# A hybrid decoder step on one core: RWKV's chunk matrices as 64-row blocks, and cache page numbers read sixteen at a time

## The reference, cut to what matters

```python
def step(S, inp):
    r_t, w_t, k_t, v_t, kk_t, a_t = inp
    sa = jnp.einsum('bhij,bhj->bhi', S, -kk_t)
    S = (S * w_t[:, :, None, :] + sa[..., None] * (kk_t * a_t)[:, :, None, :]
         + v_t[..., None] * k_t[:, :, None, :])
    return S, jnp.einsum('bhij,bhj->bhi', S, r_t)
```

```python
k_past = cache_k[l][page_table].reshape(bs, past_len, N_HEADS, HEAD_DIM)
z = jnp.einsum('bqhd,bkhd->bhqk', q, k) * (HEAD_DIM ** -0.5) + sb_bias
log_keep = jnp.where(causal, jax.nn.log_sigmoid(-z), 0.0)
after = lax.cumsum(log_keep, axis=3, reverse=True) - log_keep
A = jnp.where(causal, jnp.exp(jax.nn.log_sigmoid(z) + after), 0.0)
```

## Time and profile before

| | |
|---|---|
| median of 3 runs | 3560.51 us (3560.0 to 3560.63) |
| profiled execution, its own time | 3560.32 us |
| its span in the trace | 3558.6 us |
| TensorE busy | 3362.0 us, 94% of the span |
| VectorE, ScalarE, GpSimd busy | 27%, 13%, 17% |
| granted TensorE clock, mean | 0.97 |

### The profile page before, as it was taken

One profiled execution on the slowest core, in us unless ns is written; L12 is line 12 of the kernel. 1 busy time (PEld: TensorE's weight loads), 2 busy tenths in 40 slices (PEclk: granted clock), 3 DMA queues, 4 the chain that ended last, 5 costly groups with the idle time before them and its releaser, 6 DMA issues.

```text
span 3558.6 us, 39904 instructions
## 1 busy us (share of the span) xinstructions
PE 3362.0 (94%) x16700; PEld 2682.7 (75%) x16700; DVE 955.1 (27%) x1950; ACT 463.6 (13%) x778; POOL 600.5 (17%) x613
## 2 busy tenths in 40 slices
PE   6999998979999989999989999898799999899999
PEld 4777776657888778888857777775588877688887
DVE  3222002344333223331032220123343432333300
ACT  2001003302111111000010000123031101100000
POOL 3333000320000013440023320002200000144300
PEclk8999999989999999999989999999899999999999
DMA  6343332331110222213153433323311112122121
GB/s 265 142 153 115 121 120 75 125 98 50 45 45 30 78 83 71 83 60 105 62 213 142 155 118 113 124 82 97 98 47 45 45 45 75 71 83 83 56 82 66
DMA packets 61711, 335.27 MB, mean 94 GB/s; under 512 B 10592, under 2 KB 10976, under 8 KB 32480
## 3 DMA queue, kind: packets, MB, share of 16 engines
q1 hardware_dynamic: 46656, 295.40, 22.5%
q0 software_dynamic: 12320, 33.57, 3.1%
q10 hardware_dynamic: 2560, 3.80, 0.3%
HBM read 326.71 MB, written 6.02 MB: 94 GB/s over the span
## 4 chain that ended last, share of the span: by engine, by line
PE 86%; issue 3%; ACT 3%; DVE 3%; DMA 2%; POOLq 2%; POOL 1%; SPq 0%; DVEq 0%; ACTq 0%
PE ps L544 85%; DMA ring<-w_ada 2%; POOLq L514 1%; ACT ws L1125 1%; ACT u L1125 1%; DMA ws<-cache 1%; POOL ws L516 1%; DVE ws L1360 1%; ACT L1125 1%; DVE y L1360 0%; POOLq L516 0%; PE ps L954 0%; DVE proj L1360 0%; DVE ws L1764 0%; DVE x L1363 0%
## 5 line engine op out<-in xcount | busy, mean ns | idle before, releaser
L544 PE MATMUL ps<-u,ring 128*128 128x272 f32 x4864 | 1210.4, 400 | 57.4 <-ACT u L1125 51.1
L544 PEld LDWEIGHTS ps<-u,ring 128*128 128x128 f32 x4864 | 918.7, 193 | 283.1 <-ACT u L1125 53.8
L544 PE MATMUL ps<-proj,ring 128*128 128x272 f32 x3328 | 771.2, 394 | 9.4 <-DVE proj L1360 9.4
L544 PEld LDWEIGHTS ps<-proj,ring 128*128 128x128 f32 x3328 | 632.9, 191 | 146.9 <-DVE proj L1360 12.0
L1360 DVE TENSOR_TENSOR ws<-ws,ps 128x272 f32<-128x272 f32 (+3 forms) x570 | 269.3, 476 | 1167.1 <-PE ps L544 1158.3
L528 POOL TENSOR_TENSOR masked_room<-ring 128x512 f32<-128x512 f32 x44 | 55.8, 1267 | 1590.4 <-DMA ring<-w_up 1361.1
L544 PE MATMUL ps<-y,ring 128*128 128x272 f32 x1216 | 312.4, 393 | 0.5 <-DVE proj L1360 0.5
L1125 ACT ACTIVATE ws<-ps 128x272 f32<-128x272 f32 (+5 forms) x374 | 163.1, 443 | 1056.2 <-PE ps L544 974.3
L516 POOL DMA_DIRECT2D ws<-cache x256 | 137.5, 537 | 828.6 <-issue 828.6
L544 PEld LDWEIGHTS ps<-y,ring 128*128 128x128 f32 x1216 | 231.4, 191 | 49.8 <-DVE proj L1360 2.0
L544 PE MATMUL ps<-y,masked_room 128*128 128x272 f32 x1056 | 258.4, 395 | 0.3 <-DVE y L1360 0.2
(11 more groups left out here) (191 smaller groups left out, 1910.2 us busy)
## 6 DMA issues: line engine op xcount, KB each, us to landing
ring<-w_up SPq DMA_DIRECT2D x88, 1024.0 KB, 4.8
ring<-w_ada SPq DMA_DIRECT2D x72, 1024.0 KB, 5.3
ring<-w_down SPq DMA_DIRECT2D x64, 704.0 KB, 4.1
ws<-cache POOLq DMA_DIRECT2D x256, 128.0 KB, 2.3
ring<-w_gate SPq DMA_DIRECT2D x32, 1024.0 KB, 4.8
ring<-w_in SPq DMA_DIRECT2D x22, 1024.0 KB, 4.9
ring<-w_branch SPq DMA_DIRECT2D x32, 256.0 KB, 4.6
ring<-w_out SPq DMA_DIRECT2D x8, 1024.0 KB, 5.0
```

The lines of the kernel that those rows point to most:

```text
L544: return nc.tensor.matmul(out, lhsT, rhs, start=start, stop=stop, skip_group_check=skip)
```

## The change

There are two parts.

**Blocks of 64 rows.** The RWKV matrices are stored as 4 heads of 64 columns: rows 0 to 63 hold the block of chunk 0, rows 64 to 127 that of chunk 1, and nothing is stored of the masked halves. Each call of `heads` (4 products of 128 rows) becomes `by_chunk` (8 products of 64 rows by 64 columns, on rows 0-63 and rows 64-127 in turn, both into one PSUM bank at their own partitions) or `by_channel` (8 products whose 64 rows are the channels of one head, results of the two row halves in two banks). Because a product now reads only one head's 64 channels, `AtP`, `RtP` and `BtP` with their copies and clears are gone. The results that DVE masks and ACT copies are 256 columns instead of 512. The four transposes in groups 6 and 8 become 8 products with the identity (`turn_chunks`). In the chunk groups the products with `LakT` and `MF` take 64 rows instead of 128. The last group goes from 8 products of 128 columns to 16 of 64. The constants are cut to suit. The sample's products follow the same scheme.

**Page numbers in registers.** `cache_loads` reads the 16 page numbers of a turn before it waits for the first slot, and then for each slot waits and issues four DMAs from the registers.

```diff
                 def cache_loads(first, last):
-                    for n in range(first, last):
-                        kv, odd, hf, s = n // 16, n // 8 % 2, n // 4 % 2, n % 4
-                        pool.wait_ge(cache_used.sem, cache_used.upto(l, n - 3))
-                        for pg in range(4):
-                            at_ = (2 * s + odd) * NPAGE + (NPAGE - 1 - (4 * hf + pg))
-                            page = pool.value_load(pages[0:1, at_:at_ + 1], min_val=0, max_val=NPHYS - 1)
-                            dst = cache[:, s, pg, :]
-                            pool.dma_start(dst, cache_d[kv * (DEPTH * NPHYS) + l * NPHYS + page])\
-                                .then_inc(cache_loaded[s].sem, 16)
+                    for n0 in range(first, last, 4):
+                        numbers = [[page_number(n, pg) for pg in range(4)] for n in range(n0, n0 + 4)]
+                        for n in range(n0, n0 + 4):
+                            kv, s = n // 16, n % 4
+                            pool.wait_ge(cache_used.sem, cache_used.upto(l, n - 3))
+                            for pg in range(4):
+                                pool.dma_start(cache[:, s, pg, :],
+                                               cache_d[kv * (DEPTH * NPHYS) + l * NPHYS + numbers[s][pg]])\
+                                    .then_inc(cache_loaded[s].sem, 16)
...
-                def heads(b, lhsT, rhs, n=P, rows=P):
+                def by_chunk(b, lhsT, rhs):
                     for h in range(NH):
-                        m = mm(ps[0:rows, b, h * n:h * n + n], lhsT(h), rhs(h))
+                        for c in range(2):
+                            rows = slice(CH * c, CH * c + CH)
+                            m = mm(ps[rows, b, h * CH:h * CH + CH], lhsT[rows, h, :], rhs[rows, h, :])
                     return m
+                def by_channel(b, n, lhsT, rhs):
+                    for ft in range(2):
+                        for c in range(2):
+                            for q in range(2):
+                                r, rows, at = slice(HD * q, HD * q + HD), slice(CH * c, CH * c + CH), n * P + ft * CH
+                                m = mm(ps[rows, b + q, at:at + CH], lhsT[r, ft, rows], rhs[r, ft, rows])
+                    return m
...
-                    heads(0, ft_of(Bt), hd_of(AtP))
-                    heads(1, ft_of(At), hd_of(BtP)).then_inc(rw_pe.sem, 1)
-                    heads(2, ft_of(Kt_), hd_of(AtP))
-                    heads(3, ft_of(Bt), hd_of(RtP))
+                    by_channel(0, 0, Bt, At)
+                    by_channel(0, 1, At, Bt).then_inc(rw_pe.sem, 1)
+                    by_channel(2, 0, Kt_, At)
+                    by_channel(2, 1, Bt, Rt)
...
-                    heads(0, hd_of(MD), hd_of(ME))
-                    heads(1, hd_of(MD), hd_of(MC))
-                    heads(7, hd_of(MC), hd_of(MD)).then_inc(rw_pe.sem, 1)
+                    by_chunk(0, MD, ME)
+                    by_chunk(1, MD, MC)
+                    by_chunk(7, MC, MD).then_inc(rw_pe.sem, 1)
...
-                        heads(0, hd_of(ET), hd_of(xa))
-                        for h in range(NH):
-                            m = nc.tensor.transpose(ps[:, 1, h * P:h * P + P], xa[:, h, :], cmat(IDENT))
-                        m.then_inc(rw_pe.sem, 1)
+                        by_chunk(0, ET, xa)
+                        turn_chunks(1, xa).then_inc(rw_pe.sem, 1)
...
                             for h in (2 * ft, 2 * ft + 1):
-                                mm(ps[rows, 0, h * HD:h * HD + HD], LakT[:, h, rows],
-                                   vt[:, h * HD:h * HD + HD], start=h % 2 == 0, stop=False, skip=True)
+                                mm(ps[rows, 0, h * HD:h * HD + HD], LakT[rows, slot(h), :],
+                                   vt[rows, h * HD:h * HD + HD], start=h % 2 == 0, stop=False, skip=True)
                             m = mm(ps[rows, 0, ft * P:ft * P + P], At[:, ft, rows], sbd[:, ft, :],
                                    start=False, skip=True)
...
-                    for h in range(NH):
-                        ft, po = h // 2, HD * (h % 2)
-                        o = ps[po:po + HD, 6, 256 + ft * P:256 + ft * P + P]
-                        c2 = slice(h * HD, h * HD + HD)
-                        mm(o, sat[:, c2], MrbT[:, h, :], start=False, stop=False, skip=True)
-                        m = mm(o, vt[:, c2], MrkT[:, h, :], start=False, skip=True)
+                    for v, w in ((sat, MrbT), (vt, MrkT)):
+                        for h in range(NH):
+                            ft, po = h // 2, HD * (h % 2)
+                            for c in range(2):
+                                rows, at = slice(CH * c, CH * c + CH), 256 + ft * CH
+                                m = mm(ps[po:po + HD, 6 + c, at:at + CH], v[rows, h * HD:h * HD + HD],
+                                       w[rows, slot(h), :], start=False, stop=v is vt, skip=True)
...
-                for o, i in ((AtP, At), (RtP, Rt), (BtP, Bt)):
-                    o = o.rearrange("p (f q) n -> p f q n", f=2)
-                    for q in range(2):
-                        r = slice(64 * q, 64 * q + 64)
-                        m = V.tensor_copy(o[r, :, q, 0:n], i[r, :, 0:n])
```

More of the change, by code:

```diff
@@ L48 @@
 IN_ORDER = (8, 9, 10, 3, 0, 1, 2, 4, 5, 6, 7)
-(IDENT, ONES, BLK, TRI, CAUS, CNEG, M16U, M16L, E32L, E64L, SU64, LE64) = [P * i for i in range(12)]
-S4U = 12 * P
+(IDENT, ONES, BLK, TRI, CAUS, CNEG) = [P * i for i in range(6)]
+(M16U, M16L, E32L, E64L, SU64, LE64, ID64) = [6 * P + CH * i for i in range(7)]
+S4U = 6 * P + 7 * CH
 S4L, LE4 = S4U + TS, S4U + 2 * TS
@@ L302, in build @@
         wb = masked_room[:, :]
[L303 to L306, removed]
+        E64 = wb[:, 0:256].rearrange("p (h n) -> p h n", h=4)
+        LakT = wb[:, 256:512].rearrange("p (h n) -> p h n", h=4)
+        MrbT = wb[:, 512:768].rearrange("p (h n) -> p h n", h=4)
+        MrkT = wb[:, 768:1024].rearrange("p (h n) -> p h n", h=4)
         xtf = xt2.rearrange("p f n -> p (f n)")
@@ L889, in _, with turn_chunks, small, small_heads @@
                 fills(5, 8)
-                def heads(b, lhsT, rhs, n=P, rows=P):
+                def by_chunk(b, lhsT, rhs):
                     for h in range(NH):
-                        m = mm(ps[0:rows, b, h * n:h * n + n], lhsT(h), rhs(h))
-                    return m
[L898 to L902, removed]
+                        for c in range(2):
+                            rows = slice(CH * c, CH * c + CH)
+                            m = mm(ps[rows, b, h * CH:h * CH + CH], lhsT[rows, h, :], rhs[rows, h, :])
+                    return m
+                def by_channel(b, n, lhsT, rhs):
[5 more added lines that the diff above has]
+                    return m
+                def turn_chunks(b, v):
+                    for h in range(NH):
+                        for c in range(2):
+                            rows = slice(CH * c, CH * c + CH)
+                            m = mm(ps[rows, b, h * CH:h * CH + CH], v[rows, h, :],
+                                   cst[rows, IDENT + CH * c:IDENT + CH * c + CH])
+                    return m
+                def small(n, lhsT, rhs):
+                    for ft in range(2):
+                        for q in range(2):
+                            r, at = slice(HD * q, HD * q + HD), n * 2 * TS + ft * TS
+                            m = mm(ps[0:TS, q, at:at + TS], lhsT[r, ft, 0:TS], rhs[r, ft, 0:TS])
+                    return m
+                def small_heads(b, lhsT, rhs):
+                    for h in range(NH):
+                        m = mm(ps[0:TS, b, h * TS:h * TS + TS], lhsT[0:TS, h, 0:TS], rhs[0:TS, h, 0:TS])
+                    return m
                 for tt in range(NTT):
@@ L928, in _ @@
                     pe_.wait_ge(rw_dve.sem, tile_dve(2))
-                    heads(0, hd_of(MB), hd_of(MA))
-                    heads(1, hd_of(MA), hd_of(MB)).then_inc(rw_pe.sem, 1)
+                    by_chunk(0, MB, MA)
+                    by_chunk(1, MA, MB).then_inc(rw_pe.sem, 1)
                     piece(1)
@@ L939, in _ @@
                     pe_.wait_ge(rw_dve.sem, tile_dve(4))
-                    heads(0, hd_of(MB), hd_of(MF))
-                    heads(3, ft_of(Kt_), hd_of(RtP))
-                    heads(1, hd_of(MA), hd_of(MB)).then_inc(rw_pe.sem, 1)
+                    by_chunk(0, MB, MF)
+                    by_channel(2, 1, Kt_, Rt)
+                    by_chunk(1, MA, MB).then_inc(rw_pe.sem, 1)
                     piece(3)
@@ L945, in _ @@
                     pe_.wait_ge(rw_dve.sem, tile_dve(5))
-                    heads(0, hd_of(MC), hd_of(ME)).then_inc(rw_pe.sem, 1)
+                    by_chunk(0, MC, ME).then_inc(rw_pe.sem, 1)
                     piece(4)
@@ L972, in _ @@
                         for ft in range(2):
-                            mm(ps[:, 6, 256 + ft * P + q0:256 + ft * P + q0 + CH], sbd[:, ft, :], Rt[:, ft, rows],
```

(24 more changed lines are left out.)

115 lines of the change are left out of this document (63 added, 52 removed).

## The result

Before: 3560.57 us in this comparison. After: 3449.89 us median (3447.18 to 3452.15), ratio 0.969, interval 0.967 to 0.970: 111 us faster. The forecast was 3452.

What follows compares the result with a forecast made beforehand. PE was taken to bound the kernel, busy 94% of the span, with 55.4 us of waits for cache pages in attention. 3560.3 - 71 (page numbers) - 37 (blocks) = 3452 us, range 3437 to 3500.

Steps and rivals of the forecast that it cites:

- Part 2, -71 forecast: Attention's cache loads: reading page numbers ahead removes PE's waits and low clock, 77 us less 3 per layer; bounds -77, -50.
- what stood against the gain: Attention's page loads: contention could make pages land late in value turns 2 and 3; 3 us per layer taken off.
- The clock: Attention turns: without waits ahead of them PE keeps its full clock, gaining 10.7 us per layer, 21 for both.
- The DMA did get cheaper without the number: Rival, POOL's page loads: a DMA still takes 0.9 us without the number; gain only -36, time 3487; chance 0.08.
- its worse bound for this part: Attention: gain of only -50 us if value turns 2 and 3 each pay 4 us of late landing and keep low clock.
- Part 1, -37 forecast: RWKV tiles: overlapping 64-row products and no wait for padded copies save 4.6 us per tile, 8 tiles; bounds -51, +50.
- the 0.022 of matmuls on four tiles of the array: RWKV by_channel and last group: assumed us per matmul on four 64x64 tiles, taken between 0.0145 and 0.029.
- the wait for DVE's copies: Start of the next RWKV tile: PE no longer waits for DVE's padded copies, saving 0.28 to 0.4 us.
- The bound of -51: RWKV tiles, best case: four-way overlap at 0.0145 us per matmul and changes of shape at 0.2 instead of 0.34.
- One bank without overlap: Rival, by_chunk: both row halves writing one bank serialise at 0.058 us per matmul; +16 us, time 3505; chance 0.10.
- The clock rival: RWKV tiles: short bursts of small products drop PE's clock, 3.25 us per fall; 3582 at five per tile; chance 0.04.
- That one part does nothing: Rival, whole kernel: one of the two parts gains nothing for an unseen reason; chance 0.04, half of it above 3500 us.

Runs made afterwards that it cites:

- channel_pairs: The changed kernel with the loops of by_channel exchanged, all products of chunk 0 first, then those of chunk 1; 3451.5 us, ratio 0.969.
- chunks_in_runs: The changed kernel with the two loops of by_chunk exchanged, the 4 heads of chunk 0 first, then those of chunk 1; 3473.77 us, ratio 0.976.

## Why the prediction was right, step by step

**What bounds.** PE's own time and its waits for pages; both moved as said, and no other engine took their place.

**Part 2, -71 forecast, -67 measured.** A DMA costs 0.60 us on POOL (0.62), the loads of numbers start 0.54 apart (0.53), turns of POOL are 18.55 us apart (18.7) and PE's period is 16.7 (16.8). Turn 1 and turn 2 of layer 0 are hidden, turn 2 barely: its last DMA starts at 747.6 and lands 2.4 us later, at 750.0, and it is needed at 751.0. The forecast margin was 0.8. Turn 3 was to wait 1 us in each layer and waits 4.2 in layer 0; layer 1 waits 1.7 and 1.7. The step that is off is what stood against the gain, 3 us per layer put down to contention for bandwidth. The times to landing of the last two DMAs of turn 2 (747.5 to 748.2), then of the last three of turn 3 (768.0 to 769.5), in layer 0:

```profile
DMA to landing us min/median/max: 2.3/2.4/2.4
```

```profile
DMA to landing us min/median/max: 3.1/3.1/3.4
```

So landings did come late, by 0.7 us in one turn; that contention is why is not shown, though the DMA share stood at 0.70 then. (The last three DMAs of every other value turn, in both layers, land within 2.7 us.) What costs more is POOL's stall of 3.1 us between two DMAs, 2.6 us in which a DMA would have been issued; the rest of the 4.2, 0.9, is POOL's lag behind PE (1.1 by the forecast's terms). In layer 0 the stall lies in turn 3's own loads, in layer 1 in turn 1's (at 2441.7), which makes the two turns behind it late. It stood in the trace before at the same two DMAs, and I had not looked for it. The clock: 67.1 less the 47.7 us of waits that went leaves 19.4 for it and all else (a remainder, not a measurement), where 21 were forecast for all the turns; the turn behind the wait that stayed keeps its half clock, 1.7 us. The DMA did get cheaper without the number, so that rival is refuted (0.60, not 0.9). By the prediction's own terms its worse bound for this part is nearer to -54 than to -50: four turns at 4 us and their low clock, 7.4, off 77.

**Part 1, -37 forecast, -44 measured.** `by_chunk` costs 0.029 as assumed, a change of shape 0.14, and the chunk groups grew by 0.42 us each, 0.84 per tile as in the table. From the start of one group to the start of the next, groups 2, 3 and 5 gave -0.52, -0.93 and -0.09 against -0.52, -0.95 and -0.09. The mis-sized term is the 0.022 of matmuls on four tiles of the array: it is 0.0146. On the 64 matmuls of group 1, the 16 of `by_channel` in group 4 and the 32 of the last group that makes 112 x 0.0075 = 0.84 us per tile more, 6.7 in all, which is the difference between 37 and 44. From start to start these three gave -2.43, -1.17 and -0.45, where -1.92, -1.06 and -0.23 stood. I had taken the middle between two bounds, and the cheaper bound was right. Two small errors cancel: the wait for DVE's copies gave 0.28 of the 0.4, and group 9 gave 0.18 instead of 0.09, as the change of shape behind it was there before. The bound of -51 does not follow from its terms: 4.6 + 0.84 and nine groups at 0.14 make 6.7 per tile, -54.

**The sum.** The forecast missed the time by 2 us, closer than its parts, because part 2 brought 4 less and part 1 7 more. That is luck; the parts are good to 4 and 7 us.

**The rivals of part 1.** One bank without overlap would have shown 58 ns between starts; the two halves start 7 ns apart in one bank, so for these products, which write to different partitions, the rule of the Trainium skill ("TensorEngine Tiling (Array Packing)", Restrictions and Gotchas) does not hold here. The floor that the Trainium skill states, about 25 ns from start to start ("TensorE: Matmul & The Clock Gate", Back-to-back issue gap), does not hold from one tile of the array to the next either: four starts lie within 20 ns, and the 64 matmuls of group 1 keep up 14.6 ns each. The clock rival fell too: the tile stands at 1.00. That one part does nothing is refuted by the two runs with one part each.

## What to carry to other kernels

Small fp32 products here cost what their weights' columns cost, and several tiles of the array hide them beside each other. At full clock one matmul took 0.111 us on the full array (128 data columns), 0.058 for 64 weight columns alone (0.057 with 4 data columns), 0.029 on two tiles of the array, 0.0146 on four. Order the loops so that these tiles alternate: four instructions in a row on one cost almost nothing in `channel_pairs`, eight cost 2.7 us per tile of tokens in `chunks_in_runs`. Group products of one shape, since a change cost 0.14 us in the chunk groups, and 0.14 to 0.2 around a piece. Where an engine issues DMAs with computed addresses, take the address work out from between the release and the DMAs, and if one turn's numbers still fall between two turns, hold two turns' numbers.

## What the runs showed of the hardware that was not expected

Instructions on different tiles of the array pass each other: a matmul on a second tile starts ahead of three that stand before it in the program on the first (917.440 against 917.493 to 917.605). Which is which is inferred from spacing and duration. POOL stands still for 3.0 to 3.1 us between two DMAs twice in every run, always 104 DMAs apart. Moving the loads of the numbers did not change which DMAs (114 and 218 in all nine kernels without extra DMAs, before and after among them); 48 tiny DMAs ahead moved both by 64 places in the queue, and brought a shorter stop of 2.1 us at DMA 129. The cause is open; a busy VectorE is excluded for the stall in layer 0, where DVE did nothing.
